# Tables built four at a time, key copies and scaling moved ahead, a second store of split queries, and a quarter of the turned-weight copies given to DVE

## What is computed

```python
hn = rms_norm(h, norm_mix_g); proj = hn @ w_in
# 8 dilated heads of width 64
for window, dilation in ((128, 1), (512, 4), (2048, 16)):
    s = q @ k.T * 64**-0.5 - slope * distance        # inside the window
    o, lse = softmax(s) @ v, log_sum_exp(s)          # merged over the patterns by lse
# 8 neighbourhood heads on a 16 x 64 grid, window 8 x 16, learned bias
h = h + concat(rms(y_dil), rms(y_na)) @ w_out        # then a 16-expert MoE
...
# second block, S5 mixer
lam_bar = exp(lam * dt)                              # states are a scan with lam_bar
```

## Time and profile before

| what | us |
|---|---|
| median of three runs | 2360.04 (2358.43 to 2360.98) |
| profiled execution, its own time | 2359.11 |
| span of its trace | 2357.3 |
| PE busy, share of the span | 2163.1 (92%) |
| DVE busy | 1167.9 (50%) |
| POOL busy | 959.4 (41%) |
| ACT busy | 524.1 (22%) |

### The profile page before, as it was taken

The page is one execution under the profiler, slowest core; times in us unless marked ns, Lnnn a source line. Parts: engine busy times, 40 slices in busy tenths (PEclk is TensorE's granted clock), DMA queues, the critical chain, the costliest instruction groups (busy, mean ns, idle before and its releaser), DMA issues.

```text
span 2357.3 us, 26335 instructions
## 1 busy us (share of the span) xinstructions
PE 2163.1 (92%) x10096; PEld 1698.4 (72%) x10096; DVE 1167.9 (50%) x1927; ACT 524.1 (22%) x903; POOL 959.4 (41%) x591
## 2 busy tenths in 40 slices
PE   7979989987993999996898998899999999999997
PEld 5857779987762666664574566588888888888875
DVE  7999554545222222225688975844431342243135
ACT  3000137766321111111320023321110110011011
POOL 5643255663446657103017740343323332332324
PEclk9989989988996999998999998999999999999998
DMA  6543146655437879326422210311111111111113
GB/s 251 192 165 125 64 114 159 156 154 163 166 153 289 303 268 354 128 83 221 174 72 107 105 38 18 126 45 45 54 34 56 54 38 52 54 50 41 54 31 112
DMA packets 78961, 286.94 MB, mean 122 GB/s; under 512 B 24136, under 2 KB 24264, under 8 KB 71176
## 3 DMA queue, kind: packets, MB, share of 16 engines
q1 hardware_dynamic: 60216, 189.50, 23.8%
q10 hardware_dynamic: 11072, 57.15, 6.8%
q0 software_dynamic: 7552, 38.60, 4.5%
HBM read 212.28 MB, written 80.81 MB: 124 GB/s over the span
## 4 chain that ended last, share of the span: by engine, by line
PE 70%; DVE 17%; issue 4%; POOL 4%; DMA 3%; ACT 3%; SPq 0%; ACTq 0%; DVEq 0%; POOLq 0%
PE ps L1002 13%; PE ps L1004 13%; PE ps L1006 13%; PE ps L1256 4%; PE ps L1160 3%; PE ps L1100 3%; PE ps L1240 2%; PE ps L1236 2%; PE ps L1131 2%; PE ps L1238 2%; PE ps L1237 2%; DVE small L1971 2%; DVE work L2107 2%; DVE work L2105 1%; DVE work L2109 1%
## 5 line engine op out<-in xcount | busy, mean ns | idle before, releaser
L1002 PE MATMUL ps<-work_part 128*128 128x512 f32 x1760 | 549.5, 394 | 18.2 <-ACT work L1569 15.6
L1006 PE MATMUL ps<-work_part 128*128 128x512 f32 x1760 | 543.3, 390 | 0.0
L777 POOL CAST work_part<-ring 128x1024 fp32r<-128x1024 f32 (+2 forms) x124 | 119.6, 964 | 763.1 <-PE ps L1006 633.5
L1002 PEld LDWEIGHTS ps<-work_part 128*128 128x128 f32 x1760 | 330.5, 189 | 93.6 <-ACT work L1569 17.3
L1006 PEld LDWEIGHTS ps<-work_part 128*128 128x128 f32 x1760 | 331.3, 188 | 69.2
L1004 PE MATMUL ps<-work_part 128*128 128x512 f32 x1152 | 354.7, 389 | 0.0
L781 POOL TENSOR_TENSOR work_part<-ring,work_part 128x1024 fp32r<-128x1024 f32 (+2 forms) x124 | 282.4, 2277 | 15.9 <-PE ps L1454 6.1
L1004 PEld LDWEIGHTS ps<-work_part 128*128 128x128 f32 x1152 | 216.3, 188 | 44.8
L1004 PE MATMUL ps<-hT_part,work_part 128*128 128x512 f32 x608 | 188.9, 392 | 0.0
L2228 DVE TENSOR_TENSOR hT<-ps,hT 128x1024 f32<-128x1024 f32 x40 | 49.0, 1224 | 261.5 <-PE ps L1006 245.0
L1004 PEld LDWEIGHTS ps<-hT_part,work_part 128*128 128x128 f32 x608 | 115.3, 190 | 24.6
(11 more groups left out here) (390 smaller groups left out, 3434.7 us busy)
## 6 DMA issues: line engine op xcount, KB each, us to landing
pages<-w_moe SPq DMA_DIRECT2D x16, 2048.0 KB, 9.3
ring<-w_up_units SPq DMA_DIRECT2D x44, 512.0 KB, 3.4
w_parts<-work_part SPq DMA_DIRECT2D x36, 512.0 KB, 3.6
work_part<-w_parts SPq DMA_DIRECT2D x36, 512.0 KB, 4.0
pages<-w_moe SPq DMA_DIRECT2D x16, 1024.0 KB, 7.0
x_slots<-zeros ACTq DMA_DIRECT2D x31, 512.0 KB, 4.6
work<-x_slots ACTq DMA_DIRECT2D x31, 512.0 KB, 6.0
y_slots<-work ACTq DMA_DIRECT2D x31, 512.0 KB, 2.7
```

Of the source, the lines that this page charges most:

```text
L777: pool.tensor_copy(WHI[n % 2][:, 0:cols], w).then_inc(whi_ready, 1)
L1002: pe.matmul(ps[:, c], whi[:, w], hi[k][:, c], start=(k == 0), stop=False)
L1006: mm = pe.matmul(ps[:, c], wlo[:, w], hi[k][:, c], start=False, stop=(k == len(hi) - 1))
```

## The change

1. *Tables.* The first six doublings are done for four tables together, by TENSOR_TENSOR on a view of eight pages; the last four remain per table. Since the group writes all eight pages, the second group waits until all four first tables are stored.
2. *Scaling.* The sixteen query and key scalings come ahead of the first value scaling.
3. *Keys.* POOL makes `KL` right behind `KH`. SP does `double(1)` ahead of `load_near_values()`.
4. *Queries.* For h<8 POOL also makes `QF`, high and low queries in residue order, in ring pages 0 and 1; units q=0, 1 read their weights from it without a stride and wait for the first four parts only.
5. *Copies.* The turned weights of units with u%4=3 in dilated heads are copied by DVE, between `biased` and `head_out`.
6. `onep_ready` is folded into `rg_ready` in the second block, with counts raised by two.

```diff
+def turned_by_dve(u):
+    return u < DIL_UNITS and u % 4 == 3
...
+def parts_made(h):
+    return 6 * min(h, 8) + 4 * max(h - 8, 0)
...
+        QF = [Wr[37 + 0][:, :], Wr[37 + 1][:, :]]
...
                 own, other = halves_of(h)
-                for part, done_part in ((KH, 1), (KL, 3)):
-                    sp.wait_ge(qk_parts, 4 * h + done_part)
+                for part, done_part in ((KH, 1), (KL, 2)):
+                    sp.wait_ge(qk_parts, parts_made(h) + done_part)
...
                     double(0)
+                    double(1)
                     load_near_values()
-                    double(1)
...
                 pool.tensor_copy(KH[h % 2][own, :], k[own, :]).then_inc(qk_parts, 1)
+                pool.wait_ge(qk_parts, parts_made(h) + 1)
+                pool.tensor_tensor(KL[h % 2][own, :], k[own, :], KH[h % 2][own, :].bitcast(f32), ALU.subtract).then_inc(qk_parts, 1)
+                if h < 8:
+                    far = steps_of(q[own, :])
+                    pool.tensor_copy(residues(QF[h % 2][own, :]), far).then_inc(qk_parts, 1)
+                    pool.wait_ge(qk_parts, parts_made(h) + 3)
+                    pool.tensor_tensor(residues(QF[h % 2][other, :]), far, residues(QF[h % 2][own, :]).bitcast(f32), ALU.subtract).then_inc(qk_parts, 1)
                 pool.tensor_copy(QS[h % 2][own, :], q[own, :]).then_inc(qk_parts, 1)
-                pool.wait_ge(qk_parts, 4 * h + 2)
-                pool.tensor_tensor(KL[h % 2][own, :], k[own, :], KH[h % 2][own, :].bitcast(f32), ALU.subtract).then_inc(qk_parts, 1)
+                pool.wait_ge(qk_parts, parts_made(h + 1) - 1)
...
-                pe.wait_ge(qk_parts, 4 * (h + 1))
+                pe.wait_ge(qk_parts, parts_made(h) + 4 if h < 8 and q < 2 else parts_made(h + 1))
...
-                        lhs = queries.rearrange("p (u x r) -> p r u x", u=2, r=NR)[:, r, n % 2, :]
+                        lhs = QF[h % 2][:, n * P:(n + 1) * P]
...
-            for j in range(8):
...
+            for g in range(2):
+                if g == 1:
+                    for i in range(4):
+                        dve.wait_ge(turns_stored[i], 16)
+                both = W[:, 16:24, :].rearrange("p (j c) n -> p j c n", c=2)
...
+                for k2 in range(TOGETHER):
+                    n = 1 << k2
+                    wc, ws = (s5p[:, 5 + 2 * k2 + i, 4 * g:4 * g + 4].unsqueeze(2).unsqueeze(3).to_broadcast([P, 4, 2, n]) for i in range(2))
+                    turned = Wp[24][:, 0:8 * n].rearrange("p (j c n) -> p j c n", j=4, c=2)
+                    dve.tensor_tensor(turned, both[:, :, :, 0:n], ws, ALU.mult)
+                    link(dve.tensor_tensor(both[:, :, :, n:2 * n], both[:, :, :, 0:n], wc, ALU.mult))
+                    dve.tensor_tensor(both[:, :, 0, n:2 * n], both[:, :, 0, n:2 * n], turned[:, :, 1, :], ALU.subtract)
+                    link(dve.tensor_tensor(both[:, :, 1, n:2 * n], both[:, :, 1, n:2 * n], turned[:, :, 0, :], ALU.add))
+                for j in range(4 * g, 4 * g + 4):
...
+                    for k2 in range(TOGETHER, 10):
...
             dve.wait_ge(roots_copied, 1)
+            for m in range(8):
+                tokens, stored = (steps_of, residues) if m < 4 else (rows_of, columns)
+                for i in (m, 8 + m):
+                    dve.wait_ge(qkv_ready, i + 1)
+                    a, b = (Wp[i], RB) if i < 4 else (stored(Wp[i]), tokens(RB))
+                    dve.tensor_tensor(a, a, b, ALU.mult).then_inc(qk_scaled, 1)
             for m in range(8):
...
-                for i in (m, 8 + m):
...
+            def copy_pT(u):
+                dve.wait_ge(mm_done, done(use_t[u]))
+                dve.wait_ge(mm_done, done(use_o[u - 2]))
+                dve.tensor_copy(PT[u % 2], PS[bank(use_t[u])][:, :]).then_inc(pT_by_dve, 1)
...
                     biased(t)
+                if 0 <= t - LAG_T < NU and turned_by_dve(t - LAG_T):
+                    copy_pT(t - LAG_T)
```

More of the change, by code:

```diff
@@ L31 @@
 HEAD_ROW = DH + 2
+TOGETHER = 6
 FF = 22
@@ L63, with turned_before @@
 NU = DIL_UNITS + NA_UNITS
+def turned_by_dve(u):
+    return u < DIL_UNITS and u % 4 == 3
+def turned_before(u):
+    return sum(not turned_by_dve(v) for v in range(u)), sum(turned_by_dve(v) for v in range(u))
 def head_of(u):
@@ L1632, in _ @@
                     expo(t)
-                if 0 <= t - LAG_T < NU:
+                if 0 <= t - LAG_T < NU and not turned_by_dve(t - LAG_T):
                     copy_pT(t - LAG_T)
@@ L1771, in _ @@
             take_out(4)
-            act.wait_ge(rg_ready, 2)
+            act.wait_ge(rg_ready, 4)
             take_out(3)
@@ L2116, in _ @@
-            dve.wait_ge(roots_copied, 1)
+            for g in range(2):
[3 more added lines that the diff above has]
+                both = W[:, 16:24, :].rearrange("p (j c) n -> p j c n", c=2)
+                dve.memset(both[:, :, 0, 0:1], 1.0)
+                link(dve.memset(both[:, :, 1, 0:1], 0.0))
+                for k2 in range(TOGETHER):
+                    n = 1 << k2
+                    wc, ws = (s5p[:, 5 + 2 * k2 + i, 4 * g:4 * g + 4].unsqueeze(2).unsqueeze(3).to_broadcast([P, 4, 2, n]) for i in range(2))
[5 more added lines that the diff above has]
+                for j in range(4 * g, 4 * g + 4):
+                    ec, es = TURNS[j % 4][:, 0, :], TURNS[j % 4][:, 1, :]
+                    ta, tb = Wp[24][:, 0:HALF], Wp[24][:, HALF:S]
+                    for k2 in range(TOGETHER, 10):
+                        n = 1 << k2
+                        wc, ws = s5p[:, 5 + 2 * k2, j:j + 1], s5p[:, 6 + 2 * k2, j:j + 1]
+                        dve.tensor_scalar(ta[:, 0:n], es[:, 0:n], ws, None, ALU.mult)
+                        link(dve.tensor_scalar(tb[:, 0:n], ec[:, 0:n], ws, None, ALU.mult))
+                        dve.scalar_tensor_tensor(out=ec[:, n:2 * n], in0=ec[:, 0:n], scalar=wc, in1=ta[:, 0:n],
+                                                 op0=ALU.mult, op1=ALU.subtract)
+                        last = dve.scalar_tensor_tensor(out=es[:, n:2 * n], in0=es[:, 0:n], scalar=wc, in1=tb[:, 0:n],
+                                                        op0=ALU.mult, op1=ALU.add)
+                        if k2 < 9:
+                            link(last)
+                    last.then_inc(turns_ready, 1)
+                    dve.wait_ge(turns_ready, j + 1)
@@ L2463, in _ @@
                 dve.wait_ge(gate_steps, c + 1)
-                dve.tensor_scalar(rc, th, 1.0, None, ALU.add).then_inc(onep_ready, 1)
-                dve.wait_ge(onep_ready, c + 1)
+                dve.tensor_scalar(rc, th, 1.0, None, ALU.add).then_inc(rg_ready, 1)
+                dve.wait_ge(rg_ready, c + 1)
                 link(dve.reciprocal(rc, rc))
```

44 lines of the change are left out of this document (13 added, 31 removed).

## The result

The changed kernel took 2366.93 us (median of six runs, 2363.41 to 2373.66) against 2359.23 for the kernel before (six runs beside it). The ratio is 1.0031, 95% interval 1.0017 to 1.0044: slower by 7.7 us in the medians, by 0.17% to 0.44%. The forecast was 2383 with a range of 2353 to 2399. Direction and range held; the sum of +23 was three times too large.

What follows compares the result with a forecast made beforehand. PE, with 70% of the chain of waits, was taken as the bound. Terms +9 - 8 - 1 + 22 + 0 + 1 = +23 on the profiled 2359.1 gave 2382.1, forecast as 2383 us against the median; range 2353 to 2399.

Steps and rivals of the forecast that it cites:

- the scaling term: End of the projection: sixteen scalings ahead start the first value scaling near 250.7 instead of 242.6; about +9 us.
- the four heads: Dilated heads where DVE merges while POOL makes `QF` for a later head: 22.2 us instead of 16.7, +5.5 each, +22.
- behind the eighth store: Head 8, unit q=1: DVE's last copy delays `head_out`, on which the wait for head 9's keys hangs; +1 us.
- the start of attention: From the projection's end to head 2: two scalings gone, key copies of head 1 in time; head 2 starts 8 us sooner.
- the hold of 10 us: Projection: three POOL stretches hold DVE during the sixteen scalings, adding 10 us to their 27.8.
- Tables, end near 213: Projection: with doublings grouped for four tables, DVE leaves its tables near 213 us instead of 242.6.
- The strip of head 1: Start of attention: next to be late, since POOL works 12 us on a head; may take 0 to 3 us.
- Free periods, 15.85: A dilated head without the merge holds: bound by the chain `head_out`, key copies, scores; 15.85 us, 0.85 less than before.
- the first is held through `QF` low, the second through the CAST of `QS`, the third through `QS` low: Middle heads: POOL holds DVE's merge instructions, so DVE leaves them 9.5 us after the head's first load instead of 5.
- Rival 1: Middle heads: most merge instructions slip through POOL's gaps, the four heads cost +1, total 2362 us, no change; chance 0.09.

Runs made afterwards that it cites:

- u1: The changed kernel without the second store `QF`, units q=0 and 1 reading queries with a stride from `QS`: 2357.4 us, ratio 0.9986 to the kernel before.
- x1: The kernel before with grouped tables and the sixteen scalings ahead of the first value scaling, nothing else: 2362.7 us, ratio 1.0014.
- w4: The kernel before with the tables grouped as in the change and nothing else: 2349.0 us, ratio 0.9953.
- v1: The changed kernel with POOL's loads of the bias strips issued earlier, from head 2 on right behind `KL`: 2377.5 us, ratio 1.0087 to the kernel before.

## Why the forecast was right in direction and too large

The sum was +23, the profile shows +4.2. Of the 18.8 us between them 10.0 lie in the scaling term (+9, measured -1.0), 6.5 in the four heads and 5.6 behind the eighth store; the start of attention won 3.4 less than forecast, which works the other way. So the step that failed most is the hold of 10 us in the scaling term.

1. *Tables, end near 213.* Right: 211.8.
2. *Scaling, "+9 at the end of the projection".* The step that failed is "with three POOL stretches in it (10 us)". I had read the holds as DVE waiting for POOL alone. In fact a run of long DVE instructions with two SBUF inputs kept POOL out as well (the CAST of 17.91 us). POOL cost it 2.5 us in the profile of the change (30.3 - 27.8) and 8.4 in u1 (36.2 - 27.8). So the first value scaling started at 242.0 and not at 250.7, and PE waited 8.2 us for it and not 17. First scores came at -2.0 to -0.5 in the one kind and +3.6 to +6.0 in the other. Which of the two the profile of the change met is luck, but +9 is too much for either. Against the grouped tables alone, though, the scalings ahead cost 14 us (x1 against w4), so the term's cause was the right one to fear.
3. *Start of attention, "8 us sooner".* Right for the scores of head 1: 332.55 - 321.85 is 10.7 us behind the first scores, where it was 341.45 - 322.82 = 18.6. But from first scores to the first store of rows only 4.6 of the 8 remained. The strip of head 1, named as what is late next at 0 to 3 us, is what PE then waited for (1.88 us, through DVE). How much of the rest is this wait isn't shown: v1 has no such wait and won only 0.6 us more on this stretch, with its first scores mostly at half clock (5.01 us for them, 3.34 in the change).
4. *Free periods, 15.85.* Right: 16.0 twice.
5. *The four middle heads, "+5.5 each, +22".* Right in place, in cause for three of the four, and two fifths too large: +15.5. The part that failed is "the first is held through `QF` low, the second through the CAST of `QS`, the third through `QS` low". The forecast had five dependent instructions. But the second doesn't wait for the first: the two start 0.07 us apart, and only the later three wait for a `dve_link`. So two passed in one gap and one in the next; DVE was through the five in 4.2 us, 7.4 us after the head's first load (390.13 to 397.5) and not 9.5, and PE waited 2.8 and not 5. Rival 1 described this half. Against it, `QF` cost POOL 2.07 + 2.88 = 4.95 rather than 4.4. Two of the four heads lost more than a hold gives: one to late key copies (21.5), which I hadn't in the sum at all, and one to half clock, which lasted some 13 us behind a wait of 2.8 us in one head (23.7) and about 3 us behind an equal one in the head before (19.5).
6. *Behind the eighth store, "+1".* It was -4.6. PE waited 1.90 us there for POOL's `KL` instead of 3.14 for key copies, and half clock was shorter. A stretch whose stall hangs on when POOL's and DVE's work meet was taken as fixed.

Measured by the profile: -1.0 - 4.6 - 1.1 (free and last periods) + 15.5 - 4.6 = +4.2, the difference of the two spans; the medians differ by 7.7, and the profiled execution was the fastest of the six.

The Trainium skill, GPSIMD Engine Reference, section 8 ("Shares its SBUF interfaces with VectorE"), fits here on both sides: the copies from PSUM (L2213) took 0.41 or 0.42 us in every row of the change while merge instructions between them took up to 2.79, and POOL's CAST took 17.91 beside DVE's scalings. Section 7 of the same page of the Trainium skill puts reads with a stride of more than 8 bytes at half more. Here, with a stride of 16 bytes, it is 1.46 times in the sum of the two parts (4.95 against 1.03 + 2.36), but 2.0 times for the CAST and 1.22 for the subtraction.

## What to carry to other kernels

Where two engines keep each other waiting, cost an added instruction by what the other engine has queued at that moment and by what hangs on it: five instructions of 8 to 16 columns cost some 12 us because one `head_out` stood behind them, and one number in the order moved the time by more (20 us) than the whole change (7.7). Test a part alone and in a repaired order before judging it: grouped tables win 10 us, and the scalings put ahead of the critical one spend all of it. And try a repair on the kernel before as well: there the same edit wins 9.4 us of the 20. A profile is one execution. Where it can fall out in two ways, as the projection does here, compare stretches between marks before a difference of two medians is put down to an edit.

## What was unexpected of the hardware

- A POOL CAST of 1.04 us took 17.91 us beside back-to-back DVE scalings, while in other executions of the same instructions POOL's casts and subtractions beside them took 2.7 to 4.1 us and DVE paid 6 us more. Only these two outcomes were seen.
- Two DVE instructions of 0.16 and 0.17 us that don't wait for each other passed at the 0.1 us between two POOL instructions (393.32 in the change); the next, which waits for them, took 2.79. With 0.56 us more of POOL's time ahead (v1) the first of them met POOL's CAST in four heads and took 0.64 to 0.68.
- After equal waits of 2.8 us PE's clock stayed at half for about 3 us once and for some 13 us the next time.
